# The first stage of a hybrid decoder step: modulation weights as the moving operand, x in pieces, roots spread by a diagonal

## The chip, the cores and the metric

The kernel runs on one core of a Trainium2 chip. The metric is the device time of one execution in microseconds (us). TensorE is called PE, VectorE DVE, ScalarE ACT, GpSimd POOL; SP is the engine that only issues DMAs here.

## The reference

One decoder layer for 1024 prompt tokens and 8 decode tokens (1032 columns), D_MODEL = 1024. What matters here is its beginning: `sh1, sc1, g1, sh2, sc2, g2 = split(c @ ada_w + ada_b, 6)`, with c one vector for the prompt and eight for the decode tokens (nine in all), and `h = rms_norm(x, norm_attn) * (1 + sc1) + sh1`, then `h @ w_in`. The first stage needs only sh1 and sc1: the first 2048 columns of ada_w, 8 MB in float32. Attention, a gated linear recurrence, an output projection and a convolutional MLP follow; the change leaves them as they are.

## The kernel before

The program is a row of stages, each an `nc.Block()` in which every engine has a list of its own; all engines wait for each other at the end of a block. Nothing plans the order: it is written out by hand, with semaphores. Every large product is done in three passes over a high and a low part of each operand (`product`, L240 to 244: high by high, high by low, low by high). `high` (L232) is a cast, `low` (L237) a subtraction.

The first stage is `stage_modulation` (L313). The SP queue loads identity and c, then eight panels of ada_w of 256 columns into four buffers of `ring` (L340), the fifth and later ones when a buffer is used; then it spills xT (the channel-major x) to HBM in one DMA (L344), and loads the first group of w_in (L485). ACT's queue carries 14 loads (L354 to L367), x in one piece among them, all on one semaphore. PE (L386 to L427): turns c to `cT`; for each panel 16 products, each split by the compiler in two records, with a 128x128 block of ada_w as the weights and the nine columns of cT moving (L394); two panels, then a wait for all 14 loads, two small transposes (L403, L404), 18 groups of four transposes of x (L417) that DVE (L449) and ACT (L373) evacuate in turn through four PSUM banks; three panels; the sums of squares of the norm, all-ones weights by squared xT in 3 x 8 products of 344 columns (L268, the squares by ACT, L263); three panels. ACT takes logarithm and exponential of a 128x1032 tile for the roots (L277, L280), each with an ACT_TABLE_LOAD. DVE casts the first weight group (L232), POOL subtracts (L237), and DVE at last adds the bias (L460) and makes A1 = (1 + sc1) * gain (L467, L468).

The second stage is `stage_token_major` (L584). For each k of 8, DVE computes x * A1 * root (L306), ACT adds the shift and rounds to `hT` (L287), DVE makes the low part (L302). PE takes the first three token tiles together, k by k, as the pieces come (L697 to L702), then the other tiles of 36 units (4 weight groups by 9 tiles). ACT squares each unit, DVE reduces it (L815), multiplies by the root (L828) and the gain (L832), rotates it and marks it `normed`; PE turns unit u - 2 after unit u's products (L678, L682), the turn of unit 0 ahead of the products of unit 3. With `n_psum = 3` accumulators, PE's unit u also waits for unit u - 3 to be read. After the norm DVE casts the second weight group and POOL subtracts it.

Of the kernel before, what the change touches and what calls it, by code (L numbers as in the profile page):

```python
# [17 lines left out]
P = 128  # L18
# [50 lines left out]
def rows_of(t):  # L69

    return P if t < TT else NB
# [66 lines left out]
def allocate(nc):  # L138
# [19 lines left out]
    s.hT = sb("hT", [P, KT, TOK], F32R)  # L158
# [154 lines left out]
def stage_modulation(nc, s, T, norm, projections):  # L313
# [6 lines left out]
    panel = [view(s.ring, 2048 * i, KT, 256) for i in range(4)]  # L320
    x_in, c_in = s.sem("m_x_in"), s.sem("m_c_in")
    loaded = [s.sem(f"m_loaded{i}") for i in range(4)]
    panel_used, tr_done = s.sem("m_panel_used"), s.sem("m_tr_done")
    evac_v, evac_a, ada_done = s.sem("m_evac_v"), s.sem("m_evac_a"), s.sem("m_ada_done")
    ready = s.sem("m_cT_ready")
    ada = T["ada_w"].rearrange("(k p) n -> p k n", p=P)
    NGRP = 2 * (TT + 1)
    PANELS = G1 * P // 256
    s.spilled = s.sem("m_spilled")

    with nc.Block() as block:
        @block.sync
        def _(sp):
            sp.dma_start(s.ident[:, :], T["c_ident"]).then_inc(c_in, 16)
            sp.dma_start(c_tm[0:1, :], T["c_prompt"]).then_inc(c_in, 16)
            sp.dma_start(c_tm[1:NB + 1, :], T["c_sample"]).then_inc(c_in, 16)
            for n in range(PANELS):

                wait(sp, panel_used, n - 3)
                sp.dma_start(panel[n % 4], ada[:, :, n * 256:(n + 1) * 256]).then_inc(loaded[n % 4], 16)  # L340

# [7 lines left out]
        def _(pool):  # L349
            projections.take_low(pool, 0)  # L350

        @block.scalar
        def _(act):
            act.dma_start(rows[0:48, :], T["ada_b"][0].rearrange("(r p) -> r p", p=P)).then_inc(x_in, 16)  # L354
            act.dma_start(rows[48:56, :], T["norm_attn"][0].rearrange("(r p) -> r p", p=P)).then_inc(x_in, 16)
            act.dma_start(rows[56:64, :], T["norm_ffn"][0].rearrange("(r p) -> r p", p=P)).then_inc(x_in, 16)
            act.dma_start(rows[64:72, :], T["hg_lb"].rearrange("a (r p) -> (a r) p", p=P)).then_inc(x_in, 16)
            act.dma_start(rows[72:73, :], T["hg_norm"]).then_inc(x_in, 16)
            act.dma_start(crow[0:66, :], T["conv_w"][0].rearrange("j (r p) -> (j r) p", p=P)).then_inc(x_in, 16)
            act.dma_start(crow[66:88, :], T["conv_b"][0].rearrange("(r p) -> r p", p=P)).then_inc(x_in, 16)  # L360
            act.dma_start(x_tm[:, 0:TT, :], T["x_prompt"][0].rearrange("(t p) d -> p t d", p=P)).then_inc(x_in, 16)
            act.dma_start(x_tm[0:NB, TT, :], T["x_sample"].rearrange("b t d -> (b t) d")).then_inc(x_in, 16)
            act.dma_start(add_f, T["c_add"]).then_inc(x_in, 16)
            act.dma_start(s.rope[:, 0:TT, :], T["c_rope"][0:SEQ].rearrange("(t p) c -> p t c", p=P)).then_inc(x_in, 16)
            act.dma_start(s.rope[0:NB, TT, :], T["c_rope"][SEQ:TOK]).then_inc(x_in, 16)
            act.dma_start(s.gain[:, 0, :], T["q_gain"].partition_broadcast(P).rearrange("p a d -> p (a d)")).then_inc(x_in, 16)
            act.dma_start(s.gain[:, 1:4, :], T["k_gain"][0].partition_broadcast(P)).then_inc(x_in, 16)  # L367

            for g in range(1, NGRP, 2):
                t, half = g // 2, g % 2  # L370
                n = rows_of(t)
                act.wait_ge(tr_done, 4 + g)
                act.activation(s.xT[:, 4 * half:4 * half + 4, t * P:t * P + n],  # L373
                               view(s.ps[2 + g % 4], 0, 4, P)[:, :, 0:n], ACT.Copy).then_inc(evac_a, 1)
            act.wait_ge(x_in, 224)
            act.wait_ge(evac_v, 3 + TT + 1)
            act.wait_ge(evac_a, TT + 1)
            for k in range(KT):
                norm.square(act, k)
            norm.root(act)  # L380

        @block.tensor
        def _(pe):
# [4 lines left out]

            def modulate(n):

                pe.wait_ge(loaded[n % 4], 16 * (n // 4 + 1))
                for h in range(2):
                    for k in range(KT):
                        last = pe.matmul(s.ps[0][:, (2 * n + h) * 9:(2 * n + h + 1) * 9],  # L394
                                         panel[n % 4][:, k, h * P:(h + 1) * P], s.cT[:, k, :],
                                         start=(k == 0), stop=(k == KT - 1))
                last.then_inc(panel_used, 1)

            pe.wait_ge(ready, 1)
            for n in range(2):  # L400
                modulate(n)
            pe.wait_ge(x_in, 224)
            pe.transpose(s.ps[2][:, 0:73], rows[0:73, :], s.ident[0:73, 0:73]).then_inc(tr_done, 1)  # L403
            pe.transpose(s.ps[3][:, 0:88], crow[0:88, :], s.ident[0:88, 0:88]).then_inc(tr_done, 1)  # L404
            for g in range(NGRP):
                t, half = g // 2, g % 2
                n = rows_of(t)
                if g < 2:
                    pe.wait_ge(evac_v, 3)
                elif g >= 4:  # L410
                    if g % 2:
                        pe.wait_ge(evac_a, (g - 4) // 2 + 1)
                    else:
                        pe.wait_ge(evac_v, 3 + (g - 4) // 2 + 1)
# [5 lines left out]
            for n in range(2, 5):  # L420
                modulate(n)
            for k in range(KT):
                norm.sum(pe, k)
            for n in range(5, PANELS):
                modulate(n)
            pe.wait_ge(panel_used, PANELS)
            pe.sem_inc(ada_done, 1)  # L427

        @block.vector
        def _(v):  # L430
            ch = s.dve_chain
            v.memset(s.ones[:, :], 1.0)
            ch.link(v, v.memset(s.eps[:, :], EPS))
# [5 lines left out]
            v.wait_ge(x_in, 224)  # L439
            v.tensor_copy(s.add[:, :, :], add_f)  # L440
# [4 lines left out]
            for g in range(0, NGRP, 2):  # L445
# [5 lines left out]
            projections.take_high(v, 0)  # L451
            v.wait_ge(ada_done, 1)
            finish_modulation(s, v, 0, G1, s.ps[0])
            scale_gain(s, v, s.A1, SC1, 48)

# [15 lines left out]
class TokenMajorWeights:  # L471


    def __init__(self, s, T):
# [5 lines left out]
        self.cut, self.split = s.sem("t_cut"), s.sem("t_split")  # L480
# [9 lines left out]

    def take_low(self, pool, g):
        pool.wait_ge(self.cut, g + 1)
        low(pool, self.lo[g], self.raw[g], self.hi[g]).then_inc(self.split, 1)
# [90 lines left out]
def stage_token_major(nc, s, T, weights, norm, splits, inputs):  # L584
# [11 lines left out]
    n_psum = 3  # L596
# [7 lines left out]
    with nc.Block() as block:  # L604
        @block.gpsimd
        def _(pool):
            weights.take_low(pool, 1)
# [57 lines left out]
        def _(pe):  # L665
# [19 lines left out]
            for u in range(UNITS):  # L685
# [7 lines left out]
                if u == 0:  # L693

                    for k in range(KT):
                        pe.wait_ge(norm.ready, k + 1)
                        for first in range(n_psum):  # L697
# [5 lines left out]
                if u < n_psum:  # L703
# [10 lines left out]
        def _(act):  # L714
            ch = s.act_chain
            act.preload_act_table_set("natural_log_exp_and_others")
# [14 lines left out]
            norm.take_high(act)  # L731
# [2279 lines left out]
```

## Time and profile before

| | us |
|---|---|
| median of 3 runs | 2439.13 (2438.54 to 2445.15) |
| the profiled execution | 2445.59, its span 2443.5 |
| PE busy | 2239.8 (92%) |
| DVE, ACT, POOL busy | 1141.9, 634.7, 588.7 |
| mean granted clock of PE | 0.944 |

The times below come from the one profiled execution. In the rows, PE is a product, PEld a weight load, and PEclk the granted clock of PE as a share of full speed (1.00 is 2.4 GHz, 0.50 is 1.2 GHz). A float32 product leaves two records, one of the high and low parts (fp32r) leaves one, as the counts show. Idle time of an engine that is not the bottleneck costs nothing.

### The profile page before, as it was taken

How to read it: one execution, taken by the hardware profiler on the slowest of the kernel's cores; microseconds unless marked ns; L12 is line 12 of the kernel's file. 1: busy time of each engine (PE TensorE's matmuls, PEld its weight loads, DVE VectorE, ACT ScalarE, POOL GpSimd, SP SyncE). 2: the span in 40 equal slices, each digit the busy share in tenths (PEclk: the TensorE clock that was granted, in tenths of full speed). 3: DMA queues.
4: the chain of work that ended last, by engine and by line, in shares of the span. 5: the costliest groups of instructions: out<-in, count | busy, mean ns of one | idle time of the engine just before them, and what ended most of it. 6: DMA issues, size and time to landing. Idle time of an engine off the chain costs nothing. (4 is left out here: it accounts for less than half of the span.)

```text
span 2443.5 us, 34984 instructions
## 1 busy us (share of the span) xinstructions
PE 2239.8 (92%) x13531; PEld 2026.7 (83%) x13531; DVE 1141.9 (47%) x2116; ACT 634.7 (26%) x1344; POOL 588.7 (24%) x350
## 2 busy tenths in 40 slices
PE   7899999798887999987999997969999999999997
PEld 7678687576665699987898887969999999999996
DVE  1466266688876246763111113244544434454445
ACT  1322155576663133331000001022110111011110
POOL 0202211445552055542010002113120222212020
PEclk8799989799988999988999998989999999999998
DMA  7211143100006322212242322112111111111101
GB/s 260 87 36 64 42 156 129 70 1 1 1 2 227 131 66 54 54 45 78 62 109 71 94 58 106 35 39 70 48 40 52 35 53 35 53 40 48 52 18 72
DMA packets 164464, 164.57 MB, mean 67 GB/s; under 512 B 11026, under 2 KB 148883, under 8 KB 159748
## 3 DMA queue, kind: packets, MB, share of 16 engines
q1 hardware_dynamic: 154006, 109.74, 15.4%
q0 software_dynamic: 7552, 48.16, 5.9%
q10 hardware_dynamic: 2768, 4.70, 0.5%
q8 instruction: 102, 1.67, 0.3%
q14 instruction: 36, 0.29, 0.0%
HBM read 148.99 MB, written 17.87 MB: 68 GB/s over the span
## 5 line engine op out<-in xcount | busy, mean ns | idle before, releaser
L242 PE MATMUL psall<-hT,ring_short 128*128 128x344 f32 x1512 | 491.8, 325 | 28.6 <-DVE work_short L302 11.9
L244 PE MATMUL psall<-hT,ring_short 128*128 128x344 f32 x1512 | 486.6, 322 | 0.0
L237 POOL TENSOR_TENSOR ring_short<-ring,ring_short 128x2048 fp32r<-128x2048 f32 (+3 forms) x48 | 195.7, 4076 | 998.7 <-DVE ring_short L232 998.7
L243 PE MATMUL psall<-work_short,ring_short 128*128 128x344 f32 x1296 | 418.5, 323 | 0.0
L242 PEld LDWEIGHTS psall<-hT,ring_short 128*128 128x128 f32 x1512 | 288.0, 190 | 30.3 <-issue 23.5
L244 PEld LDWEIGHTS psall<-hT,ring_short 128*128 128x128 f32 x1512 | 287.6, 190 | 0.0
L243 PEld LDWEIGHTS psall<-work_short,ring_short 128*128 128x128 f32 x1296 | 247.5, 191 | 0.6
L2881 DVE SCALAR_TENSOR_TENSOR xT<-psall,mod,xT 128x344 f32<-128x344 f32 (+1 forms) x264 | 151.4, 573 | 129.4 <-PE psall L244 126.3
L2785 ACT ACTIVATE work<-psall 128x344 f32<-128x344 f32 (+1 forms) x66 | 30.0, 456 | 531.4 <-PE psall L244 531.3
L242 PE MATMUL psall<-work_short,work_short 128*128 128x344 f32 x480 | 160.9, 335 | 0.0
L243 PE MATMUL psall<-work_short,work_short 128*128 128x344 f32 x480 | 153.7, 320 | 0.0
L244 PE MATMUL psall<-work_short,work_short 128*128 128x344 f32 x480 | 153.6, 320 | 0.0
L243 PE MATMUL psall<-xT_short,ring_short 128*128 128x344 f32 x456 | 146.4, 321 | 0.0
L237 POOL TENSOR_TENSOR work_short<-work,work_short 128x2048 fp32r<-128x2048 f32 (+3 forms) x18 | 86.7, 4818 | 234.9 <-DVE work_short L232 234.9
L2463 DVE TENSOR_TENSOR work<-work,psall 128x344 f32<-128x344 f32 (+1 forms) x48 | 24.6, 513 | 253.3 <-PE psall L2427 253.3
L1175 POOL TENSOR_SCALAR ring<-ring,work 128x640 f32<-128x640 f32 (+7 forms) x128 | 104.7, 824 | 102.0 <-DVE work L1373 100.7
L2829 DVE SCALAR_TENSOR_TENSOR work<-work,conv 128x1024 f32<-128x1024 f32 x22 | 37.6, 1709 | 169.1 <-ACT work L2796 169.1
L1388 DVE TENSOR_TENSOR work_short<-psall,work_short 128x512 fp32r<-128x512 f32 (+1 forms) x148 | 101.0, 685 | 33.3 <-ACT work_short L1311 30.9
L1268 PE MATMUL psall<-work_short,work_short 128*128 128x512 f32 (+1 forms) x296 | 110.2, 455 | 0.0
L1311 ACT ACTIVATE work_short<-psall 128x512 fp32r<-128x512 f32 (+1 forms) x148 | 87.6, 594 | 72.1 <-PE psall L1251 44.7
L242 PEld LDWEIGHTS psall<-work_short,work_short 128*128 128x128 f32 x480 | 90.0, 188 | 14.6 <-DVE xT L2881 13.9
L1251 PE MATMUL psall<-ident,ring 128*128 128x128 f32 x528 | 84.3, 284 | 18.4 <-POOL ring L1175 9.3
(410 smaller groups left out, 4599.1 us busy)
## 6 DMA issues: line engine op xcount, KB each, us to landing
ring<-in_w_up SPq DMA_DIRECT2D x44, 512.0 KB, 5.0
ring<-in_ada_w SPq DMA_DIRECT2D x32, 512.0 KB, 4.0
work<-in_w_down SPq DMA_DIRECT2D x10, 1024.0 KB, 4.9
ring<-in_w_in SPq DMA_DIRECT2D x19, 512.0 KB, 3.8
ring<-in_ada_w SPq DMA_DIRECT2D x8, 1024.0 KB, 13.1
work<-in_w_in SPq DMA_DIRECT2D x9, 512.0 KB, 5.2
x_spill<-xT SPq DMA_DIRECT2D x1, 4128.0 KB, 15.9
xT<-x_spill SPq DMA_DIRECT2D x1, 4128.0 KB, 15.1
```

What stands on the lines that cost most here:

```text
L237: return eng.tensor_tensor(lo, src, hi, ALU.subtract)
L242: pe.matmul(out, w[0], x[0], start=first, stop=False)
L243: pe.matmul(out, w[0], x[1], start=False, stop=False)
L244: return pe.matmul(out, w[1], x[0], start=False, stop=last)
L1175: pool.tensor_scalar(p, p, recip[:, u.index % 4, j:j + 1], s.gates[:, u.t, column:column + 1], ALU.mult, ALU.mult).then_inc(normed, 1)
L1251: last = pe.transpose(turn_ps[i % 2][:, j * P:(j + 1) * P], probability(u, j)[:, (c - u.lo) * P:(c - u.lo + 1) * P], s.ident[:, :])
L1268: last = pe.matmul(out_ps[u.pair % 2], kept, split_T[i % 3][part][0:rows], start=(i == pair_first[u.pair] and part == 0), stop=(i == pair_ ...
L1311: act.activation(split_T[i % 3][0][0:rows], turn_ps[i % 2][0:rows, :], ACT.Copy).then_inc(high_done, 1)
L1388: v.tensor_tensor(lo, turn_ps[i % 2][0:rows, :], hi, ALU.subtract).then_inc(low_done, 1)
L2785: last = act.activation(u[:, 2 + c * CH:2 + c * CH + m], s.ps[c][:, 0:m], ACT.Copy)
L2829: ch.link(v, v.scalar_tensor_tensor(out=y[:, 0:SEQ], in0=u[:, 1:SEQ + 1], scalar=taps[1], in1=y[:, 0:SEQ], op0=ALU.mult, op1=ALU.add))
L2881: v.scalar_tensor_tensor(out=at, in0=ps[:, 0:m], scalar=s.mod[:, G2 + n, 0:1], in1=at, op0=ALU.mult, op1=ALU.add).then_inc(added, 1)
```

## The change

- Modulation (class `Modulation`): cT's nine columns are now the weights, and ada_w moves past them in four panels of 512 columns, each loaded in two halves of 1 MB, in the order SC1, SC1 + 4, SH1, SH1 + 4, with a buffer for each: two in `ring`, two in the space of `hT`. A panel is 8 products of 512 columns (two records each) into one row tile in PSUM. ACT copies the 9x512 result to SBUF (`move`), PE turns it back by four small transposes (`turn`), DVE adds the bias (`finish`). The panel 3 sums are in the first stage, its move, turn and finish in the second.
- Loads: x comes in four pieces on the SP queue behind panel 0, with panels 1 and 2 after it; the first weight group and panel 3 are issued when all transposes and squares are done, and then the spill, in four pieces. The rows of vectors stay on ACT's queue; the mask, rope and gain loads go to POOL's queue, and DVE waits for them (`late_in`) between the diagonal and its eight multiplications.
- Norm: ACT squares x token-major with an accumulated sum per token, takes 128x9 logarithms and exponentials; DVE multiplies the identity by each token's root into nine diagonal blocks; PE spreads them with all-ones weights over all partitions in PSUM; DVE multiplies xT by that into a new region of `work`. The 48 sum records L268 of this stage go.
- Of the 18 groups of transposes DVE evacuates 12, ACT 6.
- The high part of the first weight group is cast by ACT in two halves, the second after the move of panel 2, where DVE had cast it whole. POOL's subtraction waits for both.
- Second stage (class `FirstNorm`): DVE scales and shifts in one instruction with one source, ACT rounds, and the low parts are DVE's for even k and POOL's for odd k. Each waits for its piece of the spill. The decode columns come last.
- `n_psum` is 6; the first three tiles are still taken together (`FIRST = 3`). One table load, at the start.

```diff
@@ stage_modulation, SP
-            for n in range(PANELS):
-                wait(sp, panel_used, n - 3)
-                sp.dma_start(panel[n % 4], ada[:, :, n * 256:(n + 1) * 256]).then_inc(loaded[n % 4], 16)
-            sp.wait_ge(evac_v, 3 + TT + 1)
-            sp.wait_ge(evac_a, TT + 1)
-            sp.dma_start(T["x_spill"], s.xT[:, :, :]).then_inc(s.spilled, 16)
+            modulation.load(sp, 0, 0)
+            modulation.load(sp, 0, 1)
+            for i in range(4):
+                sp.dma_start(x_tm[:, 2 * i:2 * i + 2, :], ...).then_inc(x_in[i], 16)
+            sp.dma_start(x_tm[0:NB, TT, :], ...).then_inc(x_in[3], 16)
+            for p in (1, 2):
+                for h in range(2):
+                    modulation.load(sp, p, h)
+            sp.wait_ge(tr_done, 3 + NGRP)
+            sp.wait_ge(squared, TT + 1)
             projections.load(sp, 0)
+            for h in range(2):
+                modulation.load(sp, 3, h)
+            evacuate_all(sp)
+            norm.spill(sp, T)
@@ ACT
+            for t in range(TT + 1):
+                n = rows_of(t)
+                act.wait_ge(x_in[pair_of(t)], 32 if pair_of(t) == 3 else 16)
+                s.act_chain.link(act, act.activation(junk[0:n, :], x_tm[0:n, t, :], ACT.Square, accum_out=sums[0:n, t:t + 1]))
+                act.nop().then_inc(squared, 1)
+                for g in (2 * t, 2 * t + 1):
+                    if g in by_act:
...
+                if t == 3:
+                    modulation.move(act, 0)
+            s.act_chain.link(act, act.activation(logs, sums, ACT.Ln, bias=s.eps[:, 0:1], scale=1.0 / D))
+            act.activation(rstd, logs, ACT.Exp, scale=-0.5).then_inc(root, 1)
+            modulation.move(act, 1)
+            projections.take_first_high(act, 0)
+            modulation.move(act, 2)
+            projections.take_first_high(act, 1)
@@ PE, after the transposes of x
-            for n in range(2, 5):
-                modulate(n)
-            for k in range(KT):
-                norm.sum(pe, k)
-            for n in range(5, PANELS):
-                modulate(n)
+            modulation.sum(pe, 1, 0)
+            evacuate_all(pe)
+            pe.wait_ge(diag_ready, 1)
+            for t in range(TT):
+                pe.matmul(spread_ps[:, t * P:(t + 1) * P], s.ones[:, :], diag[:, t, :], start=True, stop=True)
+            pe.matmul(spread_dec, s.ones[:, :], diag[:, TT, 0:NB], start=True, stop=True).then_inc(spread, 1)
+            modulation.sum(pe, 1, 1)
+            modulation.sum(pe, 2, 0)
+            modulation.turn(pe, 0)
+            modulation.turn(pe, 1)
+            modulation.sum(pe, 2, 1)
+            modulation.sum(pe, 3, 0)
+            modulation.turn(pe, 2)
+            modulation.sum(pe, 3, 1)
@@ DVE, after its evacuations
+            v.tensor_tensor(diag, bc(s.ident[:, :].unsqueeze(1), ...), bc(rstd.unsqueeze(2), ...), ALU.mult).then_inc(diag_ready, 1)
+            v.wait_ge(s.late_in, 80)
+            v.tensor_copy(s.add[:, :, :], add_f)
+            evacuate_all(v)
+            v.wait_ge(spread, 1)
+            for k in range(KT):
+                v.tensor_tensor(norm.x[:, k, 0:SEQ], s.xT[:, k, 0:SEQ], spread_ps, ALU.mult)
...
+            modulation.finish(v, 0, 2)
             scale_gain(s, v, s.A1, SC1, 48)
+            modulation.finish(v, 2, 1)
@@ stage_token_major
-    n_psum = 3
+    n_psum, FIRST = 6, 3
@@ POOL
+            for k in range(1, KT, 2):
+                norm.take_low(pool, k, norm.ready_p)
             weights.take_low(pool, 1)
@@ PE, unit 0
                     for k in range(KT):
-                        pe.wait_ge(norm.ready, k + 1)
+                        norm.wait_ready(pe, k)
...
+                        if k == 0:
+                            modulation.turn(pe, 3)
@@ ACT
-            norm.take_high(act)
+            for k in range(KT):
+                if k == 4:
+                    modulation.move(act, 3)
+                norm.take_high(act, k)
@@ DVE
-            norm.scale_and_take_low(v)
+            for k in range(KT):
+                if k == 4:
+                    modulation.finish(v, 3, 1)
+                norm.scale(v, k)
+                if k % 2:
+                    norm.take_low(v, k - 1, norm.ready_v)
+            norm.decode_columns(v)
             weights.take_high(v, 1)
@@ class FirstNorm
+    def scale(self, v, k):
+        s, x = self.s, self.x[:, k, 0:SEQ]
+        v.tensor_scalar(x, x, s.A1[:, k, 0:1], s.mod[:, SH1 + k, 0:1], ALU.mult, ALU.add).then_inc(self.scaled, 1)
+    def take_low(self, eng, k, ready):
+        eng.wait_ge(self.hi_ready, k + 1)
+        eng.wait_ge(self.spilled[k // 2], 16)
+        eng.tensor_tensor(self.s.xT_r[:, k, 0:SEQ], self.x[:, k, 0:SEQ], self.s.hT[:, k, 0:SEQ], ALU.subtract).then_inc(ready, 1)
@@ class Modulation
+    def sum(self, pe, p, h):
+        wait(pe, self.moved, p - 1)
+        pe.wait_ge(self.loaded[p][h], 16)
+        for k in range(4 * h, 4 * h + 4):
+            last = pe.matmul(self.acc[p], self.s.cT[:, k, :], self.panel[p][:, k, :], start=(k == 0), stop=(k == KT - 1))
+        if h:
+            last.then_inc(self.summed, 1)
+    def move(self, act, p):
+        act.wait_ge(self.summed, p + 1)
+        act.activation(self.rows[p][0:NB + 1, :], self.acc[p], ACT.Copy).then_inc(self.moved, 1)
+    def turn(self, pe, p):
+        pe.wait_ge(self.moved, p + 1)
+        for i in range(4):
+            last = pe.transpose(self.columns[p][:, 9 * i:9 * i + 9], self.rows[p][0:NB + 1, i * P:(i + 1) * P], ...)
+        last.then_inc(self.turned, 1)
```

## Rows read from the trace of the kernel before

**Rows 1.** The page: busy times and shares, and the granted clock in 40 slices.
```profile
PE 2239.8 (92%) x13531; PEld 2026.7 (83%) x13531; DVE 1141.9 (47%) x2116; ACT 634.7 (26%) x1344; POOL 588.7 (24%) x350
...
PEclk8799989799988999988999998989999999999998
```

**Rows 2.** Timeline of the first stage: start, duration, engine, line, what [idle before it].
```profile
6.83 13.12 ACTq L365 DMA_DIRECT2D rope<-in_c_rope  x1
7.88 6.97 PE L394 MATMUL psall<-cT,ring 128*128 128x9 f32 x32 [3.38 <-DMA ring<-in_ada_w]
...
29.19 0.38 PE L403 MATMUL psall<-ident,work 73*128 73x73 f32 x1 [4.04 <-DMA gain<-in_k_gain]
...
30.47 9.87 PE L417 MATMUL psall<-ident,work 128*128 128x128 f32 x72 [0.74 <-DVEq L444]
...
40.27 16.37 PE L394 MATMUL psall<-cT,ring 128*128 128x9 f32 x96
...
56.49 16.88 PE L268 MATMUL psall<-work,ones 128*128 128x344 f32 x48
...
73.21 18.20 PE L394 MATMUL psall<-cT,ring 128*128 128x9 f32 x96
...
73.92 8.84 POOL L237 TENSOR_TENSOR work_short<-work,work_short 128x4096 fp32r<-128x4096 f32 x1 [73.47 <-DVE work_short L232]
...
92.11 0.23 DVE L468 TENSOR_TENSOR A<-A,vec 128x72 f32<-128x72 f32 x1
```

**Rows 3.** Windows of 4 us: busy time of each engine, PEclk, DMA share, GB/s.
```profile
core 0: us, PE busy (x) PEld busy (x) DVE busy (x) ACT busy (x) POOL busy (x), PEclk, DMA share, GB/s
...
8.00:12.00 4.00, 4.00 (x20) 4.00 (x20) 0.00 (x0) 0.00 (x0) 0.00 (x0) 1.00 1.04 391
...
36.00:40.00 4.00, 4.00 (x40) 3.83 (x39) 3.27 (x5) 2.62 (x6) 0.00 (x0) 1.00 0.00 0
40.00:44.00 4.00, 4.00 (x40) 3.98 (x38) 0.23 (x2) 2.59 (x4) 0.00 (x0) 1.00 0.00 0
...
48.00:52.00 4.00, 4.00 (x20) 4.00 (x21) 0.00 (x0) 0.00 (x0) 0.00 (x0) 0.50 0.32 82
...
64.00:68.00 4.00, 4.00 (x15) 2.62 (x14) 0.00 (x0) 2.19 (x3) 0.00 (x0) 1.00 0.87 346
```

**Rows 4.** Groups by line in 0 to 92.6: busy us, mean ns, idle before.
```profile
L394 PE MATMUL psall<-cT,ring 128*128 128x9 f32 x256 | 48.5, 335 | 6.7 <-DMA ring<-in_ada_w 6.7
...
L263 ACT ACTIVATE work<-xT 128x1032 f32<-128x1032 f32 x8 | 8.4, 1061 | 22.0 <-PE psall L268 21.9
...
L232 DVE CAST work_short<-work 128x4096 fp32r<-128x4096 f32 x1 | 2.3, 2295 | 31.2 <-DMA work<-in_w_in 31.2
```

**Rows 5.** Timeline of the second stage's start.
```profile
98.69 0.76 PE L242 MATMUL psall<-work_short,hT 128*128 128x512 f32 x1 [7.28 <-DVE xT_short L302]
...
106.10 0.40 PE L244 MATMUL psall<-work_short,xT_short 128*128 128x512 f32 x1
...
115.95 6.69 POOL L237 TENSOR_TENSOR ring_short<-ring,ring_short 128x3072 fp32r<-128x3072 f32 x1 [33.20 <-DVE ring_short L232]
...
117.27 0.39 PE L244 MATMUL psall<-work_short,xT_short 128*128 128x512 f32 x1
...
119.06 4.21 DVE L832 TENSOR_TENSOR work<-work,gain 128x256 f32<-128x256 f32 x2
...
124.83 1.11 PE L678 MATMUL psall<-ident,work 128*128 128x128 f32 x4 [7.17 <-DVEq L847]
```

**Rows 6.** Waits of PE from 92 to 290: us in total, times, longest.
```profile
PE psall L242 <- DVE xT_short L302: 7.3, 1, 7.3
PE psall L678 <- DVEq L847: 7.2, 1, 7.2
PE psall L682 <- DVEq L847: 5.1, 2, 2.8
```

**Rows 7.** Timeline of PE in the decode tile of the first group.
```profile
158.38 0.39 PE L244 MATMUL psall<-work_short,xT_short 128*8 128x512 f32 x1
...
163.23 0.40 PE L244 MATMUL psall<-work_short,xT_short 128*8 128x512 f32 x1
```

**Rows 8.** Groups by line and form over the span; the second is the line's own view.
```profile
L2282 DVE TENSOR_TENSOR work<-psall,work 128x1024 f32<-128x1024 f32 x4 | 4.9, 1220 | 5.9 <-ACT work L2143 5.9
...
L2194 DVE TENSOR_SCALAR work<-work x4: 818/2881/2889, 870.1 to 1043.0; 128x1032 f32<-128x1032 f32 x4
...
L302 DVE SCALAR_TENSOR_TENSOR xT_short<-xT,mod,hT 128x1024 fp32r<-128x1024 f32 x8 | 10.3, 1282 | 0.0
...
L544 POOL TENSOR_TENSOR work_short<-work,work_short 128x1024 fp32r<-128x1024 f32 x2 | 4.8, 2414 | 17.9 <-ACT work_short L539 17.9
```

**Rows 9.** DMA issues of POOL's queue: KB each, us to landing.
```profile
out_s_cf<-in_state_ffn_conv POOLq DMA_DIRECT2D x1, 88.0 KB, 4.7
```

More of the change, by code:

```diff
@@ L387, in _ @@
             last.then_inc(tr_done, 1)
[L389 to L397, printed above, removed]
             pe.wait_ge(ready, 1)
-            for n in range(2):
-                modulate(n)
-            pe.wait_ge(x_in, 224)
+            for h in range(2):
+                modulation.sum(pe, 0, h)
+            pe.wait_ge(rows_in, 112)
             pe.transpose(s.ps[2][:, 0:73], rows[0:73, :], s.ident[0:73, 0:73]).then_inc(tr_done, 1)
@@ L444, in _ @@
             v.nop().then_inc(evac_v, 1)
-            for g in range(0, NGRP, 2):
+            for g in by_dve:
                 t, half = g // 2, g % 2
@@ L581, in index, with stage_token_major @@
         v.tensor_copy(self.s.gidx[:, :], self.pages_f).then_inc(self.idx_ready, 1)
-def stage_token_major(nc, s, T, weights, norm, splits, inputs):
+def stage_token_major(nc, s, T, weights, norm, modulation, splits, inputs):
     groups, raw, w_hi, w_lo, w_loaded = weights.groups, weights.raw, weights.hi, weights.lo, weights.loaded
@@ new lines, with __init__, load, finish @@
+class Modulation:
+    def __init__(self, s, T):
+        self.s = s
+        self.ada = T["ada_w"].rearrange("(k p) n -> p k n", p=P)
+        self.chunk = (SC1, SC1 + 4, SH1, SH1 + 4)
+        self.panel = [view(s.ring, 4096 * i, KT, 512) for i in range(2)] + [view(s.h_raw, 4096 * i, KT, 512) for i in range(2)]
+        self.rows = [view(s.work, 21672 + 512 * i, 512) for i in range(4)]
+        self.acc = [s.ps[6 + p % 2][0:NB + 1, :] for p in range(4)]
+        self.columns = [s.ps[0][:, 0:36], s.ps[0][:, 36:72], s.ps[1][:, 0:36], s.ps[5][:, 0:36]]
+        self.loaded = [[s.sem(f"m_ada{p}{h}") for h in range(2)] for p in range(4)]
+        self.summed, self.moved, self.turned = s.sem("m_summed"), s.sem("m_moved"), s.sem("m_turned")
+    def load(self, sp, p, h):
+        ks, c = slice(4 * h, 4 * h + 4), self.chunk[p] * P
+        sp.dma_start(self.panel[p][:, ks, :], self.ada[:, ks, c:c + 512]).then_inc(self.loaded[p][h], 16)
+    def sum(self, pe, p, h):
[11 more added lines that the diff above has]
+        for i in range(4):
+            last = pe.transpose(self.columns[p][:, 9 * i:9 * i + 9], self.rows[p][0:NB + 1, i * P:(i + 1) * P],
+                                self.s.ident[0:NB + 1, 0:NB + 1])
+        last.then_inc(self.turned, 1)
+    def finish(self, v, p, panels):
+        first = self.chunk[p]
+        v.wait_ge(self.turned, p + panels)
+        finish_modulation(self.s, v, first, first + 4 * panels, self.s.ps[(0, 0, 1, 5)[p]])
@@ L2950, in program @@
 def program(nc, T):
     s = allocate(nc)
-    projections = TokenMajorWeights(s, T)
-    norm = Norm(s, "n1", s.A1, SH1, s.xT, s.xT_r, [view(s.work, 10760 + 1032 * i, TOK) for i in range(2)],
-                view(s.work, 12824, TOK), view(s.work, 13856, TOK), view(s.work, 14888, KT, NB), (1, 6, 7))
-    stage_modulation(nc, s, T, norm, projections)
+    projections, modulation, norm = TokenMajorWeights(s, T), Modulation(s, T), FirstNorm(s)
+    stage_modulation(nc, s, T, norm, projections, modulation)
@@ L2956, in program @@
     splits, inputs = Splits(s), CompressInputs(s, T)
-    stage_token_major(nc, s, T, projections, norm, splits, inputs)
+    stage_token_major(nc, s, T, projections, norm, modulation, splits, inputs)
     stage_compress(nc, s, T, splits, inputs)
```

146 lines of the change are left out of this document (91 added, 55 removed).

## The prediction

> **What bounds the kernel now.** The page comes first [rows 1]: TensorE (PE) is busy 92% of the span, and the granted clock is below full in the first slices, so time is won where PE waits or does slow work. The timeline of the start [rows 2] shows the first stage as PE's list: a panel's 32 records L394 at 7.88 (a second such run at 18.16), a wait until 29.19 for the load issued last on ScalarE's (ACT's) queue, transposes L417 from 30.47, three panels from 40.27, 48 sum records L268 from 56.49, three panels from 73.21; VectorE (DVE) ends the stage at 92.34. The windows [rows 3] price these. In 48 to 52 the clock is 0.50 (1.2 GHz), PE is full, and each 9-column record takes 0.2 us; in 40 to 44, at 1.00 (2.4 GHz), 0.1. In 8 to 12 they took 0.2 too, though the column says 1.00: the pace is that of half clock, and I go by the pace. So the 256 records are 48.5 us [rows 4], most at half clock. In the second stage the first product stands at 98.69 [rows 5], the 72 products of three tiles end at 117.66, and PE waits 7.17 us for the first normalised tile. The waits of PE from 92 to 290 [rows 6] are its transposes (L678, L682) waiting for DVE's marks, never a product waiting for an accumulator.
>
> So I follow one event: PE's first transpose of the second stage, at **124.83** [rows 5]. Behind it stand the same work and the same waits, bound by PE; its shift is the shift of the end.
>
> **Part 1, the sums of the modulation.** Removed: 256 records, 48.5 us. Added: 4 panels x 8 k x 2 records = 64 records of 512 columns over 9-column weights. L268, of the same type with 344 columns, ran 15 records in 4 us at clock 1.00, 0.28 each [rows 3]; so 0.42 for 512, 3.4 us for half a panel at full clock, 6.8 at half, 27 to 55 us for all. Which clock? A tile with 8-column weights and 512 columns kept full pace: the records at 158.38 and 163.23 are 21 apart, 0.231 each [rows 7]. I take full clock, with some 4.5 us at half whenever PE starts from rest or sparse work: from 98.69 the pitch is 0.43, by 106.10 it is 0.23 [rows 5].
>
> **Part 2, when data is there.** DMA moves 391 GB/s when full [rows 3], 2.7 us for 1 MB. SP's queue now holds, in this order: panel 0, landing at 7 and 9.7, four pieces of x at 12.4, 15.1, 17.8, 20.5, panels 1 and 2 from 23 to 31. The wait to 29.19 goes. PE does panel 0 from 7 to 15.7 (first 4.5 us at half clock); two small transposes and their evacuation are 1.3 (29.19 to 30.47 now), so x's transposes start at 17.
>
> **Part 3, transposes and roots.** 48 sum records, 8 squares and three table loads fall. ACT now squares token-major: 9 at 1.06 [rows 4], 1.25 with the wait on itself, beside 6 evacuations of 0.6 and the move of panel 0. From its first evacuation at 18.4 that is 7 x 1.25 + 5 x 0.6 + 0.2 + 0.6 = 12.6, to 31; DVE's 12 x 0.87 are less. PE, if this paces it down to half clock, needs 72 x 0.21 = 15.3, to 32.3. I take **32**. Root 0.8, diagonal 1.45 (1.28 for 1024 elements, [rows 8]) to 34.5; PE meanwhile does half a panel from half clock, to 37.2. Spreading is 18 short records at 0.11, to 39.2. DVE multiplies 8 x 1.22 (SBUF by PSUM, [rows 8]) to 49, beside PE.
>
> **Part 4, what ends the stage.** PE: half panel to 42.6, another to 46, turns of panels 0 and 1 to 47, half to 50.4, panel 3 to 57.8. The first weights are asked for at 32 and land at 40 (2 MB, 5.4, and some 2.5 of start). ACT casts them in two halves of 2.0 (1.06 for 1032 elements, doubled), but the second cast stands behind the move of panel 2, which waits for PE's 50.4: 51.1, then 53.1. GpSimd (POOL) then subtracts 128x4096, 8.84 us [rows 2]. Today that lies beside the last three panels; now nothing covers it. Stage end **62.1** against 92.3: 30.2 won. The spill of x follows panel 3 on the queue, its pieces landing from 49 to 57; the first is needed at 65.6: hidden.
>
> **Part 5, second stage.** After 62.1: start 0.6, memsets and gain 0.6, scale of k = 0 0.65 (a one-source DVE cast of 4096 elements took 2.3, [rows 4]; I take its rate), ACT 1.15, low part 1.28, hops: first product at 67.0 (4.9 after the stage's end; 6.35 now). Then four low parts are DVE's at 1.28 and four POOL's at 2.41 [rows 8]. Here rows speak against the change: DVE's two-source L832 at 119.06 took 4.21 for two, and went on when POOL's subtraction (115.95, 6.69 long) was over [rows 5]; the one-source L2194 took 0.818 once and 2.88 at the median [rows 8]. If they take turns: 8 x 0.65 + 4 x 1.28 + 4 x 2.41 = 20 us, some 24 with decode columns and hops. PE needs 3.8 for the first nine products, waits 2 for the turn of panel 3 (ACT moves it only after four casts of x, at 73.1), and then needs 7 x 2.1 and 2 at half clock: three tiles end at 90.7. DVE ends the norm at 87.7, casts group 1 (1.75), POOL subtracts 6.69 to 96.2, and the first unit's gain multiplication stands behind it, as now; the rest of the unit is 2.2 (122.64 to 124.83). First turn at **98.4**. From the stage's end that is 36.3 us where it is 32.5 now: 3.8 given back.
>
> The Trainium skill (SBUF — State Buffer, section "SBUF: two separate sides") says that DVE and GpSimd share a port pair as an exclusive lock held for the whole instruction, and that a DVE instruction with two SBUF inputs is caught in it. The 4.21 us for two multiplications agree. By this rule the 3.8 stand; without it they would be nothing.
>
> **Part 6, six accumulators for three.** PE never waited for one [rows 6], and a turn still stands ahead of unit 3, so the 7 us wait stays: 0, at best a fraction of 1.
>
> **Sum.** 124.83 - 98.4 = 26.4; with the slack in ACT's hops I take 27. Bounds: full clock from 11 on and no turns between DVE and POOL, first turn near 92.5, 32 won; half clock to the stage's end, rival B. The profiled execution is 2445.6 (span 2443.5 and 2.1 around it), 6.5 above the median of 2439.1; the gain holds for both: 2418.6 profiled, median **2412**.
>
> **Rivals.**
> A. DVE and POOL do not hold each other up on these forms, or DVE wins the turns: DVE ends the norm near 80, POOL's 6.69 lies under PE's products, unit 0 is ready 3 to 5 us after 90. 31.5 won, **2407.5**. Against it: [rows 5, 8]. Chance 0.2.
> B. The 9-column sums keep PE at half clock as today's panels do: panel 0 to 20.7, x to 38, then 6.8 + 3.8 + 6.8 + 6.8 + 1.5 + 6.8 to 70.5, move 0.6, cast 2.0, POOL 8.84: stage end 82, 10 won, 3.8 given back: **2433**. For it: the panels from 40.27 lose the clock between 44 and 52 [rows 3]; against it [rows 7]. 0.12.
> The Trainium skill (TensorE: Matmul & The Clock Gate, section "Part 4: PE-mode transpose") says that transposes do not bring the full clock. In 36 to 40 PE did little but transposes, 40 records in 4 us [rows 3], after standing idle before 29.19 [rows 2]: the trace disagrees. By the page the transposes of x run at half clock, which the 32 above allows already.
> C. Slower than before: five small loads move to POOL's queue, and DVE waits for all of them after the diagonal, ahead of the eight multiplications. The wait is free until about 51, then one for one; past 78 the gain is gone, past 85 the kernel is slower by 0.3%; at 88 it is **2449**. For it: these loads have short rows, and on ACT's queue one of them held its issue for 13.12 us [rows 2]. Against it: a POOL load of 88 KB lands after 4.7 [rows 9]. 0.03.
> D. The mechanism is right, and clock or order in a later stage shifts the end by more than 5 us either way: 0.1.
>
> **Chances.** Forecast 0.55 (2408.5 to 2418), A 0.2, B 0.12, C 0.03, D 0.1. The range 2403 to 2426 holds the forecast, A, most of D and a part of the way to B. A measurement of this kernel tells 0.3%, 7.3 us, from no change: faster 0.92; within it 0.05 (B with a few us more, D); slower 0.03.
>
> **What would show it.** Sum records near 0.42 and clock 1.00 from 40 on; the last transpose of x near 32; POOL's 8.84 as the last event of the first stage; first product near 67; DVE instructions of 2 us beside POOL between 66 and 90; first turn near 98. It is wrong if PE stays at 0.50 in the stage, if DVE waits for a small load, or if the second stage gives back over 8 us.

## The result, and the profile after

| | median us | ratio to before (95%) | first turn | channel mixer |
|---|---|---|---|---|
| before | 2440.8 (the runs shown: 2439.1) | | 124.8 | 700.2 |
| changed, with the prediction | 2403.97 (2394.8 to 2408.0) | 0.9842 (0.981 to 0.9874) | 91.9 | 693.1 |
| changed, second set | 2417.85 (2408.8 to 2419.8) | 0.9891 (0.9869 to 0.9913) | 92.1 | 700.8 |
| changed, third set | 2402.08 (2399.9 to 2410.8) | 0.9842 (0.9824 to 0.986) | 91.9 | 694.7 |
| before, as an experiment | 2441.69 (2436.5 to 2444.9) | 0.9999 (0.9987 to 1.001) | 121.8 | 700.0 |

"First turn" is PE's first transpose of the second stage, the event that the prediction follows; "channel mixer" is the time between the first and the last ACT evacuation L2785 of that stage (L2840 in the changed kernel), which the change does not touch. The direction was right and the gain larger: 0.9842 of the 2439.1 shown is 2400.6, just under the range of 2403 to 2426. The second set's 0.9891 is 2412.5, the forecast itself, but by luck: its first turn is as early as in the first set, and a slower channel mixer makes up for it. So there are two questions: why the first turn came 30 to 33 us earlier where 26.4 were worked out, and why one and the same kernel has sets 14 us apart.

The page of the changed kernel, its first lines and the granted clock (answers to [rows 1]):
```profile
PE 2206.0 (92%) x13325; PEld 1973.9 (82%) x13325; DVE 1152.4 (48%) x2126; ACT 632.6 (26%) x1352; POOL 601.6 (25%) x359
...
PEclk9899898999979999978999998989999999999998
```
PE is busy 33.8 us less, about what the first turn won. Windows of 4 us of the same kernel (answer to [rows 3]):
```profile
core 0: us, PE busy (x) PEld busy (x) DVE busy (x) ACT busy (x) POOL busy (x), PEclk, DMA share, GB/s
...
24.00:28.00 4.00, 2.07 (x17) 1.72 (x17) 1.43 (x3) 3.76 (x7) 0.00 (x0) 1.00 1.05 385
...
36.00:40.00 4.00, 4.00 (x11) 0.82 (x10) 4.00 (x4) 0.59 (x1) 0.00 (x0) 1.00 1.05 387
...
44.00:48.00 4.00, 4.00 (x11) 0.84 (x10) 1.84 (x5) 1.11 (x2) 0.00 (x0) 1.00 1.05 432
```
The granted clock is 1.00 to the end of the stage, also behind 24 to 28, where PE was busy only half the time while ACT was busy nearly all of it. The timeline of both stages (answers to [rows 2] and [rows 5]):
```profile
7.59 5.43 PE L3067 MATMUL psall<-ring,cT 128*9 128x512 f32 x8 [2.91 <-DMA ring<-in_ada_w]
...
18.16 5.53 PE L435 MATMUL psall<-ident,work 128*128 128x128 f32 x48 [0.63 <-DVEq L468]
...
27.43 1.22 PE L435 MATMUL psall<-ident,work 128*128 128x128 f32 x12 [0.25 <-ACT xT L402]
...
28.58 3.60 PE L3067 MATMUL psall<-ring,cT 128*9 128x512 f32 x8
...
33.62 2.02 PE L443 MATMUL psall<-work,ones 128*128 128x128 f32 x16 [1.44 <-DVE work L476]
...
43.26 7.03 PE L3067 MATMUL psall<-hT,cT 128*9 128x512 f32 x16
...
49.36 8.80 POOL L238 TENSOR_TENSOR work_short<-work,work_short 128x4096 fp32r<-128x4096 f32 x1 [44.82 <-ACT work_short L528]
...
50.56 3.60 PE L3067 MATMUL psall<-hT,cT 128*9 128x512 f32 x8
...
62.49 2.45 POOL L3030 TENSOR_TENSOR xT_short<-work,hT_short 128x1024 fp32r<-128x1024 f32 x1 [4.33 <-ACT hT_short L3025]
62.65 3.58 DVE L3021 TENSOR_SCALAR work<-work,A,mod 128x1024 f32<-128x1024 f32 x2
...
82.99 6.70 POOL L238 TENSOR_TENSOR ring_short<-ring,ring_short 128x3072 fp32r<-128x3072 f32 x1 [2.58 <-DVE ring_short L233]
...
86.27 4.03 DVE L887 TENSOR_TENSOR work<-work,gain 128x256 f32<-128x256 f32 x2
...
91.86 1.11 PE L722 MATMUL psall<-ident,work 128*128 128x128 f32 x4 [6.99 <-DVEq L902]
```
From 33.62 on the order of events is the one forecast; ahead of it, PE is done with the transposes at 28.65 and with its half panel before the diagonal is there. POOL's subtraction alone ends the first stage (58.2, PE's sums at 54.2); beside POOL's 2.45 us a pair of scales takes 3.58; the gain multiplication stands again behind POOL's 6.70 and PE waits 7.0 (7.2 before).

### The profile page after: what moved, and what is told of

Read it like the earlier page. It is cut to its first block and busy times, and to the rows that moved or that the text cites. A ratio compares the mean times of both kernels' runs of the same rounds, so it can differ in the third digit from the quotient of the medians.

```text
span 2406.2 us, 34634 instructions
## 1 busy us (share of the span) xinstructions
PE 2206.0 (92%) x13325; PEld 1973.9 (82%) x13325; DVE 1152.4 (48%) x2126; ACT 632.6 (26%) x1352; POOL 601.6 (25%) x359
## 5 line engine op out<-in xcount | busy, mean ns | idle before, releaser
L243 PE MATMUL psall<-hT_short,ring_short 128*128 128x344 f32 x1512 | 490.8, 325 | 24.3 <-DVE work_short L303 11.8
L245 PE MATMUL psall<-hT_short,ring_short 128*128 128x344 f32 x1512 | 486.3, 322 | 0.0
L243 PEld LDWEIGHTS psall<-hT_short,ring_short 128*128 128x128 f32 x1512 | 287.7, 190 | 25.2 <-issue 18.3
L245 PEld LDWEIGHTS psall<-hT_short,ring_short 128*128 128x128 f32 x1512 | 287.2, 190 | 0.0
L2840 ACT ACTIVATE work<-psall 128x344 f32<-128x344 f32 (+1 forms) x66 | 30.0, 456 | 522.3 <-PE psall L245 522.3
L1230 POOL TENSOR_SCALAR ring<-ring,work 128x640 f32<-128x640 f32 (+7 forms) x128 | 104.7, 824 | 101.3 <-DVE work L1428 99.9
L1443 DVE TENSOR_TENSOR work_short<-psall,work_short 128x512 fp32r<-128x512 f32 (+1 forms) x148 | 100.9, 684 | 34.7 <-ACT work_short L1366 32.5
L1306 PE MATMUL psall<-ident,ring 128*128 128x128 f32 x528 | 84.7, 285 | 18.2 <-POOL ring L1230 9.0
```

Of the source, the lines that this page charges most:

```text
L243: pe.matmul(out, w[0], x[0], start=first, stop=False)
L245: return pe.matmul(out, w[1], x[0], start=False, stop=last)
L1230: pool.tensor_scalar(p, p, recip[:, u.index % 4, j:j + 1], s.gates[:, u.t, column:column + 1], ALU.mult, ALU.mult).then_inc(normed, 1)
L1306: last = pe.transpose(turn_ps[i % 2][:, j * P:(j + 1) * P], probability(u, j)[:, (c - u.lo) * P:(c - u.lo + 1) * P], s.ident[:, :])
L1443: v.tensor_tensor(lo, turn_ps[i % 2][0:rows, :], hi, ALU.subtract).then_inc(low_done, 1)
L2840: last = act.activation(u[:, 2 + c * CH:2 + c * CH + m], s.ps[c][:, 0:m], ACT.Copy)
```

## The experiments

**The same kernels again.** No edit.

> The changed kernel, nothing edited. The prediction said 27 us; its trace has the first turn of the second stage at 91.86 against 124.83 (33.0 us won), and 4.3 more behind it. Theory S (stops): those 4.3 us are PE standing without an instruction where the loop of the channel mixer jumps back (stops of 2.3 to 3.3 us: four in the trace of before, two in the trace of after), a thing that comes out differently from run to run. Then the first turn is again at 91.9 within 0.5 us, the number of stops is free (0 to 4), and the span follows 2401 + about 3.5 for each stop. Rival F (fixed): the new program's layout has two stops each time, at the same passes; then the trace shows two again and the runs agree within 3 us. Ratio to before 0.984 by both.

> The kernel before, nothing edited: what the measurement tells from no change, and a second trace. Ratio 1.000. Theory S: the number of stops at the loop's jump may differ from four, and the span with it by about 3.5 us each. Rival F: four again, at 1817, 1960, 2103 and 2246.

Measured: first turn 92.1, and three stops where the first trace had two; before has four again, at the same four jumps (1809, 1952, 2095 and 2238). So the number is free in the changed kernel, against rival F, though not seen to vary in the kernel before. The totals did not fall on 2401 + 3.5 a stop (the traced one is 2416 with three), but the channel mixer did follow the stops. PE's waits from 1560 to 2360, one line each of the kernel before, the changed one and late_turn (us in total, times, longest):
```profile
PE psall L242 <- issue: 10.4, 4, 2.8
```
```profile
PE psall L243 <- issue: 5.9, 2, 3.3
```
```profile
PE psall L243 <- issue: 13.6, 4, 3.5
```
"issue" means that PE waited for nothing the profile shows. PE's loop has five passes and jumps back four times. The kernel before has the stop at each of the four jumps, here two of them:
```profile
1816.98 0.65 PE L242 MATMUL psall<-hT,ring_short 128*128 128x344 f32 x1 [2.85 <-issue]
...
1960.01 0.65 PE L242 MATMUL psall<-hT,ring_short 128*128 128x344 f32 x1 [2.83 <-issue]
```
The product behind the stop takes 0.65 us, against 0.32 in the mean. The next ones start 0.29 us apart to 1819.7 and 0.16 apart from 1820.0: the clock was at half behind the stop.

**The channel mixer without a jump.** PE's loop of five passes is written out; the other engines keep theirs.
```diff
+        if not ch and not per:
+            for i in range(GR // 2):
+                body(2 * i + 1, 1, True, True)
+                body(2 * i + 2, 0, True, True)
+            body(GR, 1, False, True)
+            return
         with eng.Fori(0, GR // 2) as i:
```

> The changed kernel with PE's loop over the channel mixer written out (five passes of the same instructions without a jump; the other engines keep their loops). In four traces the time of the channel mixer follows 684 + 1.5 x (time PE stands without an instruction at the jump): 5.9 us of it gave 693.1, 10.4 gave 700.2, 13.6 gave 704.6. Theory S: without the jump the stops of 2.3 to 3.7 us go, the channel mixer takes about 685, so 8 to 20 us less than the changed kernel, and its runs spread less than 2408 to 2420. Rival (the stop is a wait on data or weights that the profile does not name): no change, four stops at the same places; or the longer program pays for its own loading elsewhere.

Measured: channel mixer 682.7, no stop, 2396.52, ratio 0.9806 (0.9789 to 0.9824), runs within 2393.3 to 2398.5. Theory S holds. Then both kernels were written out so, and measured in one set with the changed kernel:

> The kernel before with PE's channel mixer written out. Twelve traces give its time as 682.7 + 1.6 x (time PE stands at the jump), and before stands 10.2 to 10.4 us there. Theory S: channel mixer 682.7, 16 to 17.5 us under before, near 2425, ratio 0.9930. Rival (before's stops are hidden or come back elsewhere): under 10 us.

> The changed kernel with the channel mixer written out, again. Theory S: without stops nothing is left that differs from set to set: 2396.5 within 3, ratio 0.9806 within 0.0015; and the change alone is this less before_unrolled: 29 to 33 us, as the first turns say. Rival (something else differs from set to set): 5 us or more away from 2396.5.

> The changed kernel a third time. Theory S: anywhere between 2396 (no stop) and 2420 (four), with a spread wider than that of unrolled_2; its trace lies on 682.7 + 1.6 x stops.

Measured: 2427.73, 0.9943 (0.9931 to 0.9955); 2394.52, 0.9801 (0.9788 to 0.9815); 2402.08, 0.9842. The channel mixer is 682.7 in every kernel without the jump. Against stop time, all 13 traces with the loop: 5.9 us gave 693.1; 8.1 gave 695.9; 8.2 gave 694.7; 8.6 gave 696.4; 9.1 gave 696.8; 9.7 gave 698.0; 10.2 to 10.8 gave 700.0 to 700.8; 13.4 and 13.6 gave 704.5 and 704.6. That is 682.7 + 1.6 x stops within 1.5 us. Without stops on either side the change is worth 2427.7 - 2394.5 = 33 us at the medians, where the first turns are 29.5 us apart. That before gained only 15 and not 17.5 at the median is 2.5 us that I can't place. One of its six runs, the traced one, was 2417.5, 9 us under the others, and only 22 us above the traced run of unrolled_2. From the first turn to the channel mixer's first evacuation it took 1517.7 us. The two other traces of before took 1521.4 and 1525.8 there, the five of the changed first two stages 1523.9 to 1530.1. So something else between the second stage and the channel mixer differs from run to run by several us, and whether the change itself loses a few us there is not shown.

What PE stands for can be read from the same traces. The pages list the transfers of the program's own instructions as a kind of DMA, here of the changed kernel and of late_turn:
```profile
q8 instruction: 82, 1.34, 0.2%
```
```profile
q8 instruction: 100, 1.64, 0.3%
```
With two stops there are 82 of them, with three 91 (again_after, again_after_2), with four 100: nine transfers of 16 KB for each stop. They also meet in time. At each of the 45 stops in these 13 traces such a transfer starts within 0.4 us of the moment at which PE falls idle. The 7 jumps without a stop all lie in stretches of 152 to 294 us in which that queue moves nothing. From 1915 to 2160 the changed kernel, with no stop there, has no instruction transfer; late_turn, with one, has
```profile
q8 instruction: 16, 0.26, 0.5%
```
Written out, the changed kernel has 91 and before 93 of them, spread over the whole span, and PE never stands. So the stop needs both, a jump and instructions that are not yet there. Why some passes have to load their instructions and others don't is not shown.

**One part of the change at a time, on the kernel before.** only_stream has the four panels with a buffer each, `move` and `turn`; only_loads has x in pieces behind two panels and the small loads on POOL's queue; only_roots has the token-major squares and the diagonal.
```diff
@@ only_stream, PE
-            for n in range(2):
-                modulate(n)
+            for h in range(2):
+                modulation.sum(pe, 0, h)
@@ only_loads, SP
+                if n == 1:
+                    for i in range(4):
+                        sp.dma_start(x_tm[:, 2 * i:2 * i + 2, :], ...).then_inc(x_in[i], 16)
@@ only_roots, PE
-            for k in range(KT):
-                norm.sum(pe, k)
+            for t in range(TT):
+                pe.matmul(spread_ps[:, t * P:(t + 1) * P], s.ones[:, :], diag[:, t, :], start=True, stop=True)
```

> The kernel before with one part of the change: ada_w streams past cT in four panels of 512 columns with a buffer for each, in place of 256 records of 9 columns; x, the loads of ACT's queue, the squares and sums and the roots as before. Read at the first turn of the second stage (before 124.8 and 121.8 in two traces, changed 91.9). Theory: 48.5 us of PE become 64 x 0.45 = 29, the sum records of the norm run at full clock (14 in place of 16.9), the wait to 29.2 stays: 14 to 18 us of the 30 to 33. Rival (the sums are a small part, since PE idles for data in any case): under 8 us.

> The kernel before with the loads alone reordered: x in four pieces behind the first two panels on the SP queue, mask, rope and gain on POOL's queue. Theory: PE's waits of 3.3 and 4.0 us between 14.9 and 29.2 go, and the clock stays as it was: first turn 5 to 8 us earlier. Rival (data is what bounds the first stage): 12 us or more.

> The kernel before with the roots alone changed: ACT squares token-major beside its evacuations, a diagonal and 18 short records spread the roots, ACT copies them to SBUF. 48 records of 344 columns (16.9 us) become 18 of 2 to 4 us, but ACT paces the transposes (9 x 1.3 more) and no dense run lifts the clock between the six panels, so the three that ran in 16.4 and 18.2 us take up to 20 each. Theory: 5 to 10 us. If all three parts stood for themselves, their sum would be the 30 to 33; what is missing is joint (the clock).

Measured: first turns 117.1, 116.8 and 124.0, so 5 to 8, 5 to 8, and 1 to -2 us, with before's two traces at 121.8 and 124.8 (one run each: 2437.1, 2436.2, 2447.8). only_stream fell short of its theory (14 to 18). Its timeline:
```profile
7.26 9.19 PE L2968 MATMUL psall<-ring,cT 128*9 128x512 f32 x16 [2.79 <-DMA ring<-in_ada_w]
35.66 0.38 PE L396 MATMUL psall<-ident,work 73*128 73x73 f32 x1 [19.21 <-DMA gain<-in_k_gain]
```
All 8 MB of the panels are now asked for at once, beside x on ACT's queue, and the last of ACT's 14 loads lands at 35.7 where it was 29.2: PE stands 19.2 us. only_roots shows the other side: behind sparser transposes the 9-column panels run at half clock from the start.
```profile
44.23 20.65 PE L404 MATMUL psall<-cT,ring 128*128 128x9 f32 x96
```
20.65 us for what took 16.37 [rows 2]; the granted clock is 0.50 from 44 to 64. (only_roots leaves nine evacuations with ACT beside its nine squares, where the change leaves it six, so its transposes wait more often than the changed kernel's.)

**Two parts together.** only_stream's and only_loads' edits in one kernel.

> The kernel before with two parts of the change at once: streamed sums and the order of the loads. Alone they moved the first turn from 121.8 to 124.8 down to 117.1 and 116.8, 5 to 8 us each, and in the first of them PE waited 19.2 us for x behind the panels. Theory J (joint): each part removed what hid the other; together PE has data from 7 on, x's transposes near 18, and sums at full clock: first turn 97 to 101, 21 to 27 us won. Rival (additive): 10 to 16 us, first turn 107 to 112.

Measured: first turn 99.9, 22 to 25 us won (2414.96, one run), where the parts alone sum to 10 to 16: theory J. Its timeline starts like the changed kernel's:
```profile
18.39 5.43 PE L415 MATMUL psall<-ident,work 128*128 128x128 f32 x48 [0.63 <-DVEq L444]
...
37.65 14.15 PE L269 MATMUL psall<-work,ones 128*128 128x344 f32 x48
```
The rest of the change (roots by the diagonal, the cast on ACT, the new norm of the second stage) is then worth the last 8 us, though the roots alone gave nothing. The two traces say where: stream_loads ends its first stage at 67.4, the changed kernel at 58.2, and from there to the first turn they take 32.5 and 33.7. So the roots and the cast on ACT, in the first stage, give 9.2 us, and the new norm of the second gives 1.2 back. Which part of the 9.2 is whose was not tested.

**Accumulators and the low parts.**
```diff
@@ three_banks
-    n_psum, FIRST = 6, 3
+    n_psum, FIRST = 3, 3
@@ low_on_dve: POOL
-            for k in range(1, KT, 2):
-                norm.take_low(pool, k, norm.ready_p)
@@ low_on_dve: DVE
-                if k % 2:
+                if k:
                     norm.take_low(v, k - 1, norm.ready_v)
+            norm.take_low(v, KT - 1, norm.ready_v)
```

> The changed kernel with three accumulators in place of six. The prediction gave this part 0. Theory: first turn at 91.9 within 0.5, last unit of three groups at 219.6 to 220.0 within 1. Rival: six banks take up DVE's lag in groups 2 and 3: 2 us or more lost by three.

> The changed kernel with all eight low parts of the norm on DVE and none on POOL. DVE then has 8 x 1.23 + 8 x 0.75 = 15.8 us and nobody to hold it up; PE needs 2.1 us for each k. Theory (DVE and POOL take turns on SBUF operands, as the scales of 2.0 and 2.8 us beside POOL's 2.45 show): the scales fall to 0.75 each, the three tiles end as in the changed kernel (84.7) or up to 1.5 us later, DVE ends its norm up to 3 us earlier, first turn between 89 and 92.5. Rival (POOL's half is a real gain): first turn after 94.

Measured: three_banks 92.0 and last unit 219.9, nothing, as predicted. low_on_dve has its first turn at 88.2, 3.7 us earlier, better than its theory: POOL's half of the low parts is a loss. At the last unit (DVE's last reduction of the first three groups) 1.6 us are left of it, 218.4 against 220.0, and in the time of its one run (2405.9) nothing can be told. The line view of the scale in low_on_dve, then in the changed kernel (ns min/median/max, first and last start in us):
```profile
L3020 DVE TENSOR_SCALAR work<-work,A,mod x8: 805/808/812, 59.9 to 73.5; 128x1024 f32<-128x1024 f32 x8
```
```profile
L3021 DVE TENSOR_SCALAR work<-work,A,mod x8: 801/810/2893, 59.6 to 75.7; 128x1024 f32<-128x1024 f32 x8
```
With POOL silent all eight take 0.81 us; beside it the longest takes 2.89, for one source only. DVE then casts group 1 from 77.5 in place of 81.2, so POOL's 6.7 us, and the first unit behind them, start earlier.

**Versions.** best: ACT casts first, POOL subtracts in halves, and the late turn. late_turn alone, for comparison.
```diff
@@ late_turn: PE
                 if u < FIRST:
-                    turn(u - 2)
                     continue
...
                 last.then_inc(mm, 1)
+                if u == FIRST:
+                    turn(0)
                 turn(u - 2)
@@ cast first: ACT
             projections.take_first_high(act, 0)
-            modulation.move(act, 2)
             projections.take_first_high(act, 1)
+            modulation.move(act, 2)
@@ subtraction in halves: POOL, group 0
-            pool.wait_ge(self.first_cut, 2)
+            for half in range(2):
+                ks = slice(4 * half, 4 * half + 4)
+                pool.wait_ge(self.first_cut, half + 1)
+                last = low(pool, self.lo[0][:, ks, :], self.raw[0][:, ks, :], self.hi[0][:, ks, :])
...
```

> The changed kernel, but PE takes unit 3's products ahead of the turn of unit 0, which the six accumulators allow (unit 3 has its own). Theory: PE's wait of 7.0 us for the first normalised tile holds 5.6 us of products plus the slow clock behind the wait (about 2): the second stage is 6 to 7.5 us shorter, ratio about 0.981. Rival: ACT's evacuation of unit 0 now stands longer behind PE's products, DVE's units come later and the wait moves to the next turn: under 2 us won.

> Late turn, and beside it two edits at the end of the first stage: ACT casts both halves of the first weights ahead of the move of panel 2, and POOL subtracts them half by half. Theory: POOL's 8.8 us start at 44 and end near 52.7 in place of 58.2; PE's last sums (54.2) end the stage: 4 us on top of late_turn's 6 to 7.5, so 10 to 11.5 us under the changed kernel, ratio about 0.980. Rival: the barrier or the spill's last piece (needed by the low parts) takes the 4 us back: about as late_turn.

> All that held: the changed kernel with the cast first, the subtraction in halves, the late turn, and PE's channel mixer without a jump. The first three brought the first turn from 92.1 to 88.0 with PE busy ahead of it, 4.8 us at the last unit; the fourth alone gave a channel mixer of 682.7. Theory: both add: 2396.5 less about 6, near 2391, ratio about 0.978. Rival: the stops return elsewhere or the gains overlap: as unrolled, 0.9806.

> Unrolled, cast first, subtraction in halves, all low parts on DVE, no late turn. Theory: POOL's half cost 3.7 us at the first turn and 1.6 at the last unit, the late turn gave nothing at the last unit, so 4.8 + 1.6 under unrolled: near 2390 and 1 to 2 under best_unrolled (0.9783), ratio 0.977 to 0.978. Rival (the 3.7 hold to the end): 0.976 or less.

late_turn won nothing: its last unit is at 219.6, and the changed kernel's at 219.6 to 220.1. PE's waits for normalised tiles from 58 to 255 in it:
```profile
PE psall L722 <- DVEq L903: 5.5, 2, 3.8
```
The 7.0 us became 5.5 in two pieces, since the turn of unit 1 still stood right behind. best has its last unit at 214.8, 4.8 us earlier, from the other two edits: POOL starts at 43.9 and PE's sums end the stage at 54.6. Its median is 2407.92 (0.9854); its trace (2411.6) has 13.4 us of stops. best_unrolled: 2388.41, 0.9783 (0.9769 to 0.9796). last_best: 2385.56, 0.9772 (0.9759 to 0.9784), first turn at 83.6, the fastest here, though at the last unit (213.5 against 213.8) and in the ratio the two can't be told apart. In last_best's set the changed kernel stands at 2402.08 and unrolled_2 at 2394.52: 7.6 of its 16.5 us are the loop, 9.0 the edits of the first two stages, of which the last unit shows 6 to 7.

## Why the prediction was right or wrong

*What bounds the kernel and the shape of the new stage*: right. Panel 0 at 7.59 (7), transposes from 18.2 (17), last square at 31.2 and the weights asked for at 31.5 (32), POOL last in the stage, no data wait of weight, spill hidden. The sign "last transpose near 32" failed: it ended at 28.65.

*Clock of the sums* (full, not half): right; 32 records of panels 1 and 2 took 0.44 (0.42). Rival B is out.

*"PE meanwhile does half a panel from half clock, to 37.2"*: wrong, and the first mis-sized term. That half panel ran from 28.58 to 32.18, 3.60 us, where I had it from 32 to 37.2. It began 3.4 us earlier, because PE's last transposes did not wait for ACT's last squares (the squares did end at 31.2), and it took 1.6 us less, because the clock was full. The diagonal, ready at 33.5 (34.5), was then the later of the two, and the spreading ended at 35.8 (39.2). Everything behind it moved up: second move at 46.9 (50.4), POOL 49.4 to 58.2 (53.2 to 62.0). Term: 3.9 us. I let "sparse work" cost the clock without a row for it, and took ACT's pace for PE's.

*"3.8 given back" in the second stage*: the mechanism right, the size too large. From the stage's end to the first turn it is 91.86 - 58.2 = 33.7 where 36.3 were worked out and 32.5 stood before: 1.2 given back. DVE's norm and decode columns took 59.6 to 81.2, 21.6 us where I had 24. I had priced the turns at POOL's four subtractions in full, 4 x 2.41 = 9.6 us. The three pairs of scales that ran beside POOL took 3.58, 2.61 and 3.62 us against 1.54 for a pair alone, and the decode columns' first multiplication 2.43 against 0.22 (both alone in low_on_dve): 7.4 us. PE's tiles took 21.8 from the first product where I had 23.7, since the clock came back at 72.5, but that does not count: PE then waited 7.0 us for DVE.

Together 98.4 - 91.9 = 6.5 us, and the first turn stood at 91.9 to 92.7 in all five traces of the first two stages as changed. It came even ahead of the bound of the prediction, 92.5, which had no turns between DVE and POOL in it.

*"Its shift is the shift of the end"*: it holds to the last unit, which moved from 249.9 to 253.3 to 219.6 to 220.1, but is wrong as a rule for one run. Behind the first turn the channel mixer lost 10.4 to 22 us to stops and the slow clock behind them, in kernels where the code there is unchanged. In the traced run of the result it was 7.1 us better than before's, in the second set 0.6 worse. In the traced pair the spans are 37.3 us apart: 33.0 at the first turn, 7.1 in the channel mixer, and some 3 lost elsewhere. That is rival D by its shape, with 4.3 us in this pair where I gave it more than 5. In before it stood open as "issue" waits of PE on L242 (10.4 us, above); I read PE's waits of 92 to 290 only.

*Six accumulators: 0*. Right. *Loads on POOL's queue hidden* (rival C): right, DVE did not wait. Rival A, no lock, is out by the scale's 2.89.

What is open: before's first turn is at 121.8 and 122.1 in two traces and 124.8 in the first, where the last three panels ran 18.20 us against 15.31 in again_before; and between the second stage and the channel mixer the traces differ by several us (attention over the prompt 310 to 313, over the decode tokens 117 to 121, recurrence 276 to 281). None was tested.

## What to carry to other kernels

When a PE-bound stretch is rebuilt, test its parts in pairs: two parts worth 5 to 8 us each gave 22 to 25 together, and the rest, of which the roots were worth nothing alone, 8 more. Alone, the streamed sums ended in a wait for x of 19.2 us, and the roots left the old panels at half clock. An edit that moves work from DVE to POOL must be priced with DVE's own instructions on SBUF stopped for most of POOL's time: here 7.4 us beside four subtractions of 2.45 to 2.50. And before a change of 1% is measured, the stops of the bounding engine that belong to no wait should be summed over the whole span. Here they account for 7.7 us between the traced runs of two sets of one kernel whose medians are 14 us apart; the runs that were not traced can't be split so.

## What the runs showed of the hardware

- PE stands for 2.3 to 3.7 us at the jump of a loop of about 140 us of products, at some jumps and not at others; then runs at half clock. Written out, five passes have no such stop, and the channel mixer goes from 693 to 705 down to 682.7. All 45 stops go with a transfer of 16 KB of instructions that starts within 0.4 us of them; none of the 7 jumps without a stop has one.
- PE's granted clock stayed at 1.00 through a stretch with PE busy 2.07 of 4 us (24 to 28).
- A one-source DVE instruction from SBUF to SBUF is held up by POOL's subtraction (0.81 alone, 2.89 beside it). The Trainium skill (SBUF — State Buffer, section "SBUF: two separate sides") names this for DVE instructions in a 2-port mode; the 2.89 us agree, though no run here shows in which mode this instruction runs.
